# The front of a hybrid decoder layer: two token blocks enter the projections without their row factor, products are taken k-outermost, and the front gets a new order

## The reference, cut to what matters

```
h = RMSNorm_pre(x)                       # x: 2048 tokens x 2048 features per core
P = h @ W_in                             # 7168 columns: xA | gA | u | v | gB | q | gC
yA = PoolMixer(xA) * silu(gA)            # mixer A: 4 groups of 256 channels, windows 2, 4, 8, 16
yB = SGU(u, v) * silu(gB);  yC = MemXAttn(q, RMSNorm(mem) @ W_kv) * silu(gC)
x  = x + RMSNorm_post(concat(RMSNorm(yA), RMSNorm(yB), RMSNorm(yC)) @ W_out)

PoolMixer, group g, window w:  d_t = mean(xA over t-w+1..t) - xA_t ;  y = d @ pool_w[g] ; y * scale
RMSNorm(x) = x * rsqrt(mean(x*x) + eps) * gain          # one row factor for each token
```

## Time and profile before

| | |
|---|---|
| median of 3 runs | 1323.22 us (1321.9 to 1323.98) |
| the profiled execution's own time | 1322.69 us |
| its span (slowest core, core 1) | 1320.9 us |
| spans of the 8 cores | 1315.3 to 1320.9 us |
| TensorE busy | 1235.4 us, 94% of the span |
| DVE, ACT, POOL busy | 536.9, 430.7, 147.9 us |

### The profile page before, as it was taken

One profiled execution on the slowest core, in us unless ns is written; L12 is line 12 of the kernel. 1 busy time (PEld: TensorE's weight loads), 2 busy tenths in 40 slices (PEclk: granted clock), 3 DMA queues, 4 the chain that ended last, 5 costly groups with the idle time before them and its releaser, 6 DMA issues.

```text
span 1320.9 us, 17453 instructions; the slowest of 8 cores (1315.3 to 1320.9 us)
## 1 busy us (share of the span) xinstructions
PE 1235.4 (94%) x6258; PEld 574.9 (44%) x6258; DVE 536.9 (41%) x879; ACT 430.7 (33%) x783; POOL 147.9 (11%) x197
## 2 busy tenths in 40 slices
...
PEclk7797899999999999999999999999999999999998
...
GB/s 245 247 104 64 64 21 166 134 65 65 1 169 171 153 52 64 1 65 0 64 1 0 104 25 64 1 65 0 96 89 103 60 82 145 165 163 77 44 175 240
DMA packets 29924, 119.38 MB, mean 90 GB/s; under 512 B 3152, under 2 KB 9552, under 8 KB 25296
## 3 DMA queue, kind: packets, MB, share of 16 engines
...
HBM read 164.93 MB, written 29.36 MB: 147 GB/s over the span
## 4 chain that ended last, share of the span: by engine, by line
PE 81%; DVE 7%; DMA 6%; issue 3%; ACT 2%; DVEq 0%; POOL 0%; POOLq 0%; SPq 0%; ACTq 0%
PE ps L362 80%; DMA arena<-wst 4%; DVE arena L437 3%; DMA arena<-xT 2%; DVE arena L418 1%; ACT arena L428 1%; DVE arena L540 1%; DVE arena L966 1%; DVE arena L471 1%; PE ps L709 1%; DVE arena L994 0%; PE ps L519 0%; DVE arena L546 0%; ACT arena L462 0%; ACT arena L497 0%
## 5 line engine op out<-in xcount | busy, mean ns | idle before, releaser
L362 PE MATMUL ps<-arena 128*128 128x512 bf16 (+3 forms) x5922 | 1228.9, 368 | 66.6 <-ACT arena L428 53.4
L362 PEld LDWEIGHTS ps<-arena 128*128 128x128 bf16 x5922 | 560.4, 98 | 711.4 <-issue 99.2
L494 ACT ACTIVATE arena<-arena 128x512 bf16<-128x512 f32 x96 | 68.8, 716 | 399.8 <-DVE arena L858 173.6
L966 DVE SCALAR_TENSOR_TENSOR arena<-ps,arena 128x512 f32<-128x512 f32 x128 | 95.7, 750 | 164.9 <-PE ps L362 161.2
L512 POOL TENSOR_TENSOR arena<-arena 128x512 bf16<-128x512 bf16 x44 | 50.6, 1150 | 678.0 <-ACT arena L497 585.0
L970 ACT ACTIVATE ps<-arena 128x512 f32<-128x512 f32 x64 | 38.5, 602 | 223.3 <-PE ps L362 149.3
L369 POOL DMA_DIRECT2D arena<-wst x120 | 66.1, 571 | 308.2 <-PE ps L362 279.8
L540 DVE TENSOR_TENSOR arena<-arena 128x512 f32<-128x512 f32 (+5 forms) x80 | 64.2, 803 | 79.8 <-ACT arena L534 74.8
L852 DVE SCALAR_TENSOR_TENSOR arena<-ps,arena 128x512 f32<-128x512 f32 x32 | 24.0, 751 | 155.4 <-PE ps L362 63.8
L656 DVE CAST arena<-ps 128x512 bf16<-128x512 f32 x32 | 22.1, 692 | 101.6 <-PE ps L362 98.8
L497 ACT ACTIVATE arena<-arena 128x512 bf16<-128x512 f32 x96 | 58.8, 613 | 0.0
...
## 6 DMA issues: line engine op xcount, KB each, us to landing
arena<-wst POOLq DMA_DIRECT2D x120, 512.0 KB, 12.7
...
```

Source lines behind the costliest of these rows:

```text
L362: return lambda e: e.matmul(out, lhsT=lhsT, rhs=rhs, start=start, stop=stop)
L494: P.op("act", lambda e: e.activation(out=yT[:, c, tb * 512:(tb + 1) * 512], in_=tmp[ti][:], func=AF.Copy, scale=cp[:, CP_GBR + c:CP_GBR + ...
L966: P.op("dve", lambda e: e.scalar_tensor_tensor(out=ra, in0=pv, scalar=sc(c), in1=ra, op0=ALU.mult, op1=ALU.add), reads=[bk(b), ("rbr", br) ...
```

## The change

- **Blocks 0 and 1 go in raw.** `x_raw` writes `hT` as x times gain, without the row factor, on DVE (for block 1 half of slices 4 to 15 on ACT). The units (0,0) and (0,1) are run on that; their eight products are multiplied by the row factor `rst[tb]` on DVE on the way out of PSUM (`xa_evict` and `gate_evict` with `raw`; Silu then reads the result from SBUF). Later `x_norm` writes the normalised values over the raw ones: block 0 while unit (0,1) runs, block 1 in (1,0) and (1,1).
- **k outermost.** Unit (0,1) is run piece by piece of x (four slices on all four slots), and (1,1), (0,2) and (0,3) (`stream`) slice by slice: each slice k goes to four PSUM banks that are held for the unit, and `x_norm` for slice k + 5 is issued ahead of it. Units (1,0), (1,2) and (1,3) (`unit`) keep one bank for a slot, in two halves of 8 matmuls. Squares are taken in halves of a piece, and their sums, `a_chain` and the pooling parts (`pp`) are put at written places in a unit.
- **The row factor** is now Ln and then Exp with scale -0.5 on ACT; the reciprocal on DVE is gone. The halo is normalised by two DVE instructions instead of 16.
- **Loads.** Block 1 of x lands in the half of `hT` that blocks 2 and 3 will take (in runs of 2 KB), after weight chunk 2 of A0; A1 waits for piece 2 of block 1, block 2 of x for chunk 2 of A1. Keys and values weights 1 are loaded ahead of A2, and the two `emit_kv` of a pair change places.
- **Group 0** (window 2): mean and subtraction become one subtraction, and the 0.5 goes into the pooling weights. Two more buffers of `tmp` are used for odd blocks.

```diff
+    XB = {0: [0, 1, 2, 3], 2: [4, 5, 0, 1], 3: [2, 3, 4, 5]}
+
+    def x_v(tb, pc):
+        return hF[:, pc * 4:pc * 4 + 4, 512:1024] if tb == 1 else xp[XB[tb][pc]][:]
...
-    xtok = []
-    for i in range(6):
-        xtok.append(load_x(i))
-        if i == 3:
-            dma_sp(cp[:], cp_d, writes=["cp"], sem="d_c0")
-            dma_sp(xh[:].rearrange("p k t -> p (k t)"), xhT_d, writes=["xh"], sem="d_c1")
-            dma_sp(cinv[:].rearrange("p g t -> p (g t)"), cinv_d, writes=["cinv"], sem="d_c2")
-            dma_sp(ident[:], ident_d, writes=["ident"], sem="d_c3")
-    load_group(("A", 0), waits=[xtok[2]])
-    dma_pool(poolw[:].rearrange("p g c d -> p (g c d)"), poolw_d, writes=[M_T], sem="d_c4")
-    load_group(("A", 1))
-
-    def rstd_bc(b, n):
-
-        P.op("act", lambda e: e.activation(out=rstx[:, 0:n], in_=psb(b, 0, n), func=AF.Sqrt, bias=sc(ST_EPS),
-                                           scale=1.0 / D), reads=[bk(b), "eps"], writes=[M_ws])
-        P.op("dve", lambda e: e.reciprocal(out=rstx[:, 0:n], in_=rstx[:, 0:n]), reads=[M_ws], writes=[M_ws])
+    dma_sp(cp[:], cp_d, writes=["cp"], sem="d_c0")
+    dma_sp(xh[:].rearrange("p k t -> p (k t)"), xhT_d, writes=["xh"], sem="d_c1")
+    x0 = [load_x(0, pc) for pc in range(4)]
+    dma_sp(cinv[:].rearrange("p g t -> p (g t)"), cinv_d, writes=["cinv"], sem="d_c2")
+    dma_sp(ident[:], ident_d, writes=["ident"], sem="d_c3")
+    load_group(("A", 0), waits=[x0[2]])
...
+    def rstd_bc(b, n, dst, M):
+
+        P.op("act", lambda e: e.activation(out=dst, in_=psb(b, 0, n), func=AF.Ln, bias=sc(ST_EPS),
+                                           scale=1.0 / D), reads=[bk(b), "eps"], writes=[M])
+        P.op("act", lambda e: e.activation(out=dst, in_=dst, func=AF.Exp, scale=-0.5), reads=[M], writes=[M])
...
+    def x_raw(tb, k, eng="dve"):
+        o_ = hT[:, k, tb * 512:(tb + 1) * 512]
+        i_ = x_v(tb, k // 4)[:, k % 4, :]
+        g_ = cp[:, CP_GPRE + k:CP_GPRE + k + 1]
+        r, w = [x_M(tb, k // 4, k % 4, 1), "cp"], [M_hT(tb, [k])]
+        if eng == "act":
+            P.op("act", lambda e: e.activation(out=o_, in_=i_, func=AF.Copy, scale=g_), reads=r, writes=w)
+        else:
+            P.op(eng, lambda e: e.tensor_scalar(out=o_, in0=i_, scalar1=g_, scalar2=None, op0=ALU.mult),
+                 reads=r, writes=w)
+
+    def x_norm(tb, k, eng="dve"):
+        P.op(eng, lambda e: e.scalar_tensor_tensor(
+            out=hT[:, k, tb * 512:(tb + 1) * 512], in0=x_v(tb, k // 4)[:, k % 4, :],
+            scalar=cp[:, CP_GPRE + k:CP_GPRE + k + 1], in1=rst[tb][:], op0=ALU.mult, op1=ALU.mult),
+            reads=[x_M(tb, k // 4, k % 4, 1), M_rst[tb], "cp"], writes=[M_hT(tb, [k])])
...
+    def xa_evict(g, cc, tb, b, raw):
+        X_ = xa[g % 2][cc]
+        MX = M_xa[g % 2][cc]
+        if raw:
+            P.op("dve", lambda e: e.tensor_tensor(out=X_[:, 16:528], in0=psb(b), in1=rst[tb][:], op=ALU.mult),
+                 reads=[bk(b), M_rst[tb]], writes=[MX])
+        else:
+            P.op("act", lambda e: e.copy(out=X_[:, 16:528], in_=psb(b)), reads=[bk(b)], writes=[MX])
...
+        if g == 0:
+            P.op("dve", lambda e: e.tensor_tensor(out=dv, in0=X_[:, 15:527], in1=X_[:, 16:528], op=ALU.subtract),
+                 reads=[MX], writes=[Md])
...
+    def gate_evict(tb, dc, b, raw, ts):
+        if raw:
+            P.op("dve", lambda e: e.tensor_tensor(out=tmp[ts + dc][:], in0=psb(b), in1=rst[tb][:], op=ALU.mult),
+                 reads=[bk(b), M_rst[tb]], writes=[M_tmp[ts + dc]])
+            P.op("act", lambda e: e.activation(out=tmp[ts + dc][:], in_=tmp[ts + dc][:], func=AF.Silu),
+                 reads=[M_tmp[ts + dc]], writes=[M_tmp[ts + dc]])
+        else:
+            silu(b, ts + dc)
...
-    norm_x(0)
...
+    def block_sums(tb):
+        b, todo = [0], {}
+
+        def sq(i):
+            if i == 0:
+                b[0] = bank(True)
+            todo[i] = x_square(tb, b[0], i // 2, i % 2)
+
+        def sm(i):
+            todo.pop(i)()
+            if i == 7:
+                rstd_bc(b[0], 512, rst[tb][:], M_rst[tb])
+                release(b[0])
+        return sq, sm
...
     norm_halo()
-    norm_x(1)
-    a_block(0, 0, True)
-    a_block(0, 1, True)
-    norm_x(2)
-    a_block(1, 0)
-    norm_x(3)
-    a_block(1, 1)
-    a_block(0, 2)
-    norm_mem()
-    a_block(0, 3)
+    sq0, sm0 = block_sums(0)
+    for i in range(8):
+        sq0(i)
+        x_raw(0, 2 * i)
+        x_raw(0, 2 * i + 1)
+        if i:
+            sm0(i - 1)
+    sm0(7)
+    x1 = [load_x(1, pc, waits=[wtok[("A", 0, 2)]] if pc == 0 else ()) for pc in range(4)]
+    dma_pool(poolw[:].rearrange("p g c d -> p (g c d)"), poolw_d, writes=[M_T], sem="d_c4", waits=[x1[2]])
+    load_group(("A", 1))
+
+    for s in range(4):
+        b = bank()
+        proj(s, 0, b)
+        if s < 2:
+            a_halo(0, s)
+            xa_evict(0, s, 0, b, True)
+            a_chain(0, s, 0)
+        else:
+            if s == 3:
+                for k in range(4):
+                    x_raw(1, k)
+            gate_evict(0, s - 2, b, True, 0)
+
+    sq1, sm1 = block_sums(1)
+    bs = [bank(True) for _ in range(4)]
+    for pc in range(4):
+        if pc:
+            for k in range(pc * 4, pc * 4 + 4):
+                x_raw(1, k, "dve" if k % 4 < 2 else "act")
+            sm1(2 * pc - 2)
+            sm1(2 * pc - 1)
+        sq1(2 * pc)
+        sq1(2 * pc + 1)
+        for k in range(pc * 4, pc * 4 + 4):
+            x_norm(0, k)
+        for s in range(4):
+            proj(s, 1, bs[s], range(pc * 4, pc * 4 + 4))
+    for pc in range(4):
+        load_x(2, pc, waits=[wtok[("A", 1, 2)]] if pc == 0 else ())
+    for pc in range(2):
+        load_x(3, pc)
+    P.op("dve", lambda e: e.tensor_scalar(out=poolw[:, 0], in0=poolw[:, 0], scalar1=0.5, scalar2=None,
+                                          op0=ALU.mult), reads=[M_T], writes=[M_T])
+    sm1(6)
+    sm1(7)
+
+    def unit(g, tb, at, chain=True):
+        r0 = halves[("A", g)] * 4
+        ts = 2 * (tb % 2)
+
+        def do(p):
+            for f in at.get(p, ()):
+                f()
+        for s in range(4):
+            b = bank()
+            proj(r0 + s, tb, b, range(0, 8))
+            do(2 * s)
+            proj(r0 + s, tb, b, range(8, 16))
+            if s < 2:
+                if tb == 0:
+                    a_halo(g, s)
+                xa_evict(g, s, tb, b, False)
+                if chain:
+                    a_chain(g, s, tb)
+            else:
+                gate_evict(tb, s - 2, b, False, ts)
+            do(2 * s + 1)
+
+    def stream(g, tb, at, k0=0):
+        r0 = halves[("A", g)] * 4
+        ts = 2 * (tb % 2)
+        bs = [bank(True) for _ in range(4)]
+        for k in range(k0, 5):
+            x_norm(tb, k)
+        for k in range(16):
+            if k + 5 < 16 and k + 5 >= k0:
+                x_norm(tb, k + 5)
+            for s in range(4):
+                proj(r0 + s, tb, bs[s], range(k, k + 1))
+            for f in at.get(k, ()):
+                f()
+        for s in range(2):
+            xa_evict(g, s, tb, bs[s], False)
+        for s in range(2):
+            gate_evict(tb, s, bs[2 + s], False, ts)
+        release(*bs)
+
+    def C(f, *a):
+        return lambda: f(*a)
+
+    def N(tb, lo, hi):
+        return [C(x_norm, tb, k) for k in range(lo, hi)]
+
+    def gates1():
+        for dc in range(2):
+            gate_evict(1, dc, bs[2 + dc], True, 2)
+        release(*bs)
+
+    sq2, sm2 = block_sums(2)
+    def pp(g, tb):
+        flush()
+        pool_part(g, tb, 2 * (tb % 2))
+
+    unit(1, 0, {0: [C(xa_evict, 0, cc, 1, bs[cc], True) for cc in range(2)] + [gates1],
+                2: N(1, 0, 3), 3: [C(pp, 0, 0)], 4: N(1, 3, 6) + [C(a_chain, 0, cc, 1) for cc in range(2)],
+                6: N(1, 6, 9) + [C(a_chain, 1, 0, 0), C(sq2, 0), C(sq2, 1)],
+                7: [C(sm2, 0), C(sq2, 2), C(sm2, 1), C(sq2, 3)]}, False)
+    stream(1, 1, {0: [C(sm2, 2), C(sq2, 4)], 1: [C(sm2, 3), C(sq2, 5)], 2: [C(sm2, 4), C(sq2, 6)],
+                  4: [C(a_chain, 1, 1, 0), C(sm2, 5), C(sq2, 7)], 6: [C(sm2, 6)], 7: [C(sm2, 7)],
+                  8: [C(pp, 0, 1)]}, 9)
+    sq3, sm3 = block_sums(3)
+    stream(0, 2, {0: [C(pp, 1, 0)], 1: [C(a_chain, 1, 0, 1)], 3: [C(a_chain, 1, 1, 1)], 5: [C(sq3, 0)], 6: [C(sq3, 1)],
+                  7: [C(sm3, 0)],
+                  8: [C(sm3, 1), C(sq3, 2)], 9: [C(sq3, 3)], 10: [C(sm3, 2)], 11: [C(pp, 1, 1)], 12: [C(sm3, 3)]})
+    for pc in range(2, 4):
+        load_x(3, pc)
+    load_mem()
+    unit(1, 2, {0: [C(sq3, 4)] + [C(a_chain, 0, cc, 2) for cc in range(2)], 1: [C(sq3, 5), C(sm3, 4)],
+                2: [C(sq3, 6), C(sm3, 5)], 3: [C(sq3, 7), C(sm3, 6)],
+                4: [C(sm3, 7), C(pp, 0, 2)]})
+    ms = {}
+
+    def msq(i):
+        ms[i] = mem_square(i // 2, i % 2)
+
+    def msm(i):
+        ms.pop(i)()
+        if i == 3:
+            rstd_bc(mbank[0], 256, rst[0][:, 0:256], M_rst[0])
+            release(mbank[0])
```

(17 more changed lines are left out.)

250 lines of the change are left out of this document (144 added, 106 removed).

## The result

The changed kernel takes 1267.2 us (median; 1266.47 to 1267.24) against 1323.2 before: ratio 0.9577, 95% interval 0.9558 to 0.9596, 56 us faster. In some executions, whatever the kernel, the cores of one die show a lower clock and the time is longer (1510.34 us once for the changed kernel, 1554.45 once for the kernel before, three of four in e4): they are left out of every comparison of times, and the trace of e4 is read on a core of the other die. Forecast were 1264 and 1256 to 1280.

A forecast was written before the change was run, and what follows sets the result against it. It took TensorE's idle time and low clock in the front as the bound. 139.9 of work plus losses gave 163.6 against 224.1, 60.5 less; 59.0 after 1.5 for unit changes, so 1322.7 becomes 1264 us, range 1256 to 1280.

The forecast's parts named there:

- The bound and the sum: TensorE's idle time and low clock in the front: at most 84.2 us to win; terms sum to 163.6, 60.5 less.
- the mark: First one-column products in unit (2,0), at 224.1 us before, same work ahead in both kernels; forecast at 163 to 166.
- hand-overs: Seven changes of unit up to (2,0) at 0.2 us each: 1.5 us added, so 59.0 us gained.
- the start: Ahead of unit (0,0): first slot at 21.2 us after 4.1 us of work, 17.1 lost, and 1.9 at half clock.
- (0,1): Second unit, 38 to 57 us: ACT's raw slices end at 43.5, TensorE asks at 42.4; 1.2 us lost with the hand-over.
- the walk: Unit-by-unit costing of the change by what makes TensorE wait, (0,0) to (1,3); 1256 to 1269 us, chance 0.60.
- (1,0): Third unit, to 72.4 us: A1's chunk 0 there at 51, slot 3 starts at 69; no wait.
- (0,2): Unit ending at 111.5 us: two waits, 2.1 us for ACT's first gate and 1.4 for DVE's slices.
- Edits at no price: Reciprocal removed from a path with slack, table loads covered by DVE idle 88 to 93; without cover 1.3 us, once.
- Late data: Block 1's 2 KB runs take up to double 3.3 us a piece: 1270; chance 0.30 together with blocking queues.
- Queues that block each other: ACT's and DVE's fixed order costs four k-outermost units 2 to 4 us each: 1272 to 1280; 0.30 with late data.
- The clock: Short waits hold TensorE at half clock in k-outermost units: 55 us more, 1319, or 1360; chance 0.04.

The follow-up runs named there:

- e4: Kernel before with one move, norm_x(1) issued behind unit (0,0) and not ahead of it: 1338.8 us, a single execution.
- e6: Changed kernel with pp(1, 0) in unit (0,2) issued after slice 3 and not after slice 0: 1266.95 us.
- e10: Changed kernel with pp(1, 0) in (0,2) behind slice 3, two squares of block 3 ahead of it, raw gates of (0,1) evicted in slot 1 of (1,0): ratio 0.9551.
- e3: Changed kernel with the row factor by Sqrt on ACT and reciprocal on DVE again, in place of Ln and Exp: 1281.5 us.
- e9: Changed kernel with all squares and sums of block 1 issued ahead of unit (0,0) again, raw entry and loads kept: 1289.7 us.
- e2: Changed kernel with slots outermost in (1,1), (0,2) and (0,3), all normalisations of a block issued ahead: 1281.4 us.
- e8: Changed kernel with block 1 normalised before it enters unit (0,1), block 0 still raw: 1279.1 us.

## Why the prediction was right, and where it was off

**The bound and the sum.** That TensorE's idle time and low clock in the front are all that can be won, and that the gain stays, was right: 56.1 us at the mark (60.5 in the sum, 59.0 with the allowance for hand-overs), 1097.4 behind it against 1096.8. Term by term the forecast of the mark was 139.9 + 17.1 + 1.9 + 1.2 + 2.1 + 1.4 + 1.5 = 165.1, and measured is 139.9 + 19.8 + 1.8 + 1.5 + 1.3 (a wait that was not forecast, in (1,0)) + 1.3 + 1.4 + 0.5 (another, in (0,3)) + 0.6 for the rest = 168.1. Most of the 3.0 are the start.

**The start, mis-sized.** I had the first slot at 21.2; it came at 23.85, so 19.8 us were lost in place of 17.1. Piece 3 of block 0 was in at 18.8, not 18.0; A0 was issued 0.6 later, chunk 0 came 5.0 us behind that piece, not 3.2, and the next two chunks took 3.7 us each (chunk 2, which releases SP, was in at 31.3). The price of 3.2 was read in the earlier trace rows at 165 GB/s; at 24 to 32 us the weights move at 142 to 150.

**(0,1).** I found 1.2 us lost to ACT's raw slices. Measured are 1.47 at its first slice, waited for by DVE from the load: piece 0 of block 1 landed at 40.2, where I had 34. It was issued at 31.3, 3.8 later than in the walk, and took 8.9 us to land, where the walk had 6.5. Right in size by luck, wrong in cause.

**(1,0), a miss.** "No wait": there is one of 1.26, for the copy of slot 0. ACT had the two gates of (0,1) ahead of it, which wait for the factor of block 1 and need a table load. I had followed DVE there and not ACT. ACT's rows:

```profile
59.79 1.28 ACT L444 ACT_TABLE_LOAD   x1 [2.73 <-PE ps L380]
...
64.96 1.28 ACT L636 ACT_TABLE_LOAD   x1 [2.47 <-DVE arena L634]
66.26 1.15 ACT L636 ACTIVATE arena<-arena 128x512 f32<-128x512 f32 x2
...
67.55 0.59 ACT L586 COPY arena<-ps 128x512 f32<-128x512 f32 x1
```

**(0,2).** The bank that Silu frees late cost 1.32 (2.1 forecast), DVE's slices 0.38 + 1.05 (1.4 forecast). The places are right. e6 adds that TensorE also meets ACT's order there, e10 that what is left is a wait for DVE.

**Not in the walk:** 0.53 in (0,3) for a bank. Start and waits together are the 3 us by which 1264 was low.

**Edits at no price: wrong.** That the reciprocal "goes from a path that now has slack" was checked for (0,2) alone and for 1.3 us. e3 shows 12.2 us at the mark, half waits and half the clock that they set off: the slack does not cover 3.35 us in each factor. Nor was the table load free everywhere, as the prediction had it. In (1,0) two of them, 1.28 us each, stand between the sums of block 1 and the copy that TensorE waits 1.26 us for; no run took them out.

**The rivals.** Late data: e9 gives 3.2 us a piece in short runs, so this rival falls (for these runs of 2 KB the trace agrees with the Trainium skill, DMA: Bandwidth & Descriptors, Specifications, that runs of 512 B and more reach line rate; of shorter ones they tell nothing). Queues that block each other: 6.0 us of waits behind the first slot, none above 1.5, where this rival had 8 to 16 more than the walk's 4.7. The clock: it did not go down in the k-outermost units, and 36 matmuls of (1,1), from 88.00 us, took 7.93 us, 0.22 apiece, so going through four banks costs nothing here. But the mechanism is close: in e2, e3 and e8 a few more waits of 0.8 to 3.9 us brought it down.

**What brought the 56 us.** Each taken out alone, raw entry of block 0 is worth 12.2, of block 1 11.9 (half of it the clock), the place of block 1's sums 22.5, k-outermost in three units 14.2, Ln and Exp 14.3. That is 75, more than the whole 56: the parts need each other, and none of these prices is a share. The reorder alone in the old kernel costs 16. The shorter normalisation of the halo, group 0's shorter chain and the order of the loads behind the front were not run by themselves.
